# Gate/up of a SwiGLU in Strassen's form over both halves of the tokens, and a down product with the contraction outermost

## The reference

```python
def swiglu(h, w_gu, w_down):
    g, u = jnp.split(h @ w_gu, 2, axis=-1)
    return (jax.nn.silu(g) * u) @ w_down
```

## Time and profile before

| | |
|---|---|
| median of 3 runs | 1446.25 us (1444.8 to 1448.13) |
| span of the profiled execution | 1446.7 us |
| TensorE busy (matmuls) | 1404.5 us, 97% |
| weight loads | 1149.9 us, 79% |
| VectorE, ScalarE, GpSimd busy | 746.3, 553.0, 613.6 us |
| DMA | 156.67 MB, 108 GB/s over the span |
| granted TensorE clock, mean | 0.992 |

### The profile page before, as it was taken

One profiled execution on the slowest core, in us unless ns is written; L12 is line 12 of the kernel. 1 busy time (PEld: TensorE's weight loads), 2 busy tenths in 40 slices (PEclk: granted clock), 3 DMA queues, 4 the chain that ended last, 5 costly groups with the idle time before them and its releaser, 6 DMA issues.

```text
span 1446.7 us, 20394 instructions
## 1 busy us (share of the span) xinstructions
PE 1404.5 (97%) x7753; PEld 1149.9 (79%) x7753; DVE 746.3 (52%) x1023; ACT 553.0 (38%) x864; POOL 613.6 (42%) x291
## 2 busy tenths in 40 slices
PE   5999999999998999999999999999999999999997
PEld 1589667899987888888788888888888888888886
DVE  6764657893946887447745542145446411120122
ACT  4672644322214777644432223232232233233221
POOL 3353122061436554383444444444445444444442
PEclk9999999999999999999999999999999999999999
DMA  9852111414203545443233333333333433332332
GB/s 325 311 174 72 50 44 29 132 30 131 59 30 103 139 137 148 147 147 100 73 94 96 88 101 101 89 94 105 94 98 91 143 101 96 94 100 82 94 100 89
DMA packets 236451, 156.67 MB, mean 108 GB/s; under 512 B 10532, under 2 KB 221874, under 8 KB 236252
## 3 DMA queue, kind: packets, MB, share of 16 engines
q1 hardware_dynamic: 234387, 148.70, 34.1%
q10 hardware_dynamic: 1992, 6.99, 1.3%
HBM read 147.25 MB, written 8.81 MB: 108 GB/s over the span
## 4 chain that ended last, share of the span: by engine, by line
PE 88%; DVE 4%; ACT 3%; issue 1%; DVEq 0%
PE ps L1925 36%; PE ps L1930 18%; PE ps L2093 11%; PE ps L2098 6%; PE ps L2256 2%; PE ps L2233 1%; PE ps L2194 1%; PE ps L2111 1%; ACT pr L998 1%; PE ps L2140 1%; PE ps L2152 1%; PE ps L1987 1%; PE ps L1974 1%; PE ps L1994 1%; PE ps L2236 1%
## 5 line engine op out<-in xcount | busy, mean ns | idle before, releaser
L1131 POOL TENSOR_TENSOR w_lo<-raw,w_hi 128x1024 fp32r<-128x1024 f32 x152 | 376.0, 2474 | 440.8 <-ACT w_hi L708 440.8
L1925 PE MATMUL ps<-hb_hi,w_hi 128*128 128x512 f32 x768 | 300.9, 392 | 1.6 <-DVE hb_lo L1791 1.6
L1925 PE MATMUL ps<-hb_lo,w_hi 128*128 128x512 f32 x768 | 299.1, 390 | 0.0
L708 ACT ACTIVATE w_hi<-raw 128x1024 fp32r<-128x1024 f32 x152 | 160.0, 1053 | 168.0 <-PE ps L1930 163.1
L1930 PE MATMUL ps<-hb_hi,w_lo 128*128 128x512 f32 x768 | 192.2, 392 | 0.0
L1151 POOL TENSOR_TENSOR w_lo<-raw,w_hi 128x1024 fp32r<-128x1024 f32 x21 | 89.1, 4245 | 219.8 <-ACT w_hi L862 219.8
L1925 PEld LDWEIGHTS ps<-hb_hi,w_hi 128*128 128x128 f32 x768 | 144.3, 188 | 33.2 <-DVE hb_lo L1791 3.4
L1930 PEld LDWEIGHTS ps<-hb_hi,w_lo 128*128 128x128 f32 x768 | 145.1, 189 | 31.7 <-issue 1.4
L1925 PEld LDWEIGHTS ps<-hb_lo,w_hi 128*128 128x128 f32 x768 | 144.3, 188 | 29.8 <-issue 0.2
L2093 PE MATMUL ps<-ha_hi,w_hi 128*128 128x512 f32 (+2 forms) x432 | 163.5, 379 | 3.1 <-ACT p_hy L869 2.8
L2093 PE MATMUL ps<-ha_lo,w_hi 128*128 128x512 f32 (+2 forms) x432 | 161.2, 373 | 0.0
(11 more groups left out here) (296 smaller groups left out, 2107.2 us busy)
## 6 DMA issues: line engine op xcount, KB each, us to landing
raw<-in_ffn_w_gu SPq DMA_DIRECT2D x88, 512.0 KB, 3.8
ada1x<-in_ada_w SPq DMA_DIRECT2D x32, 512.0 KB, 3.9
raw<-in_ffn_w_down SPq DMA_DIRECT2D x32, 512.0 KB, 3.8
raw<-in_w_in SPq DMA_DIRECT2D x22, 512.0 KB, 4.0
ada<-in_ada_w SPq DMA_DIRECT2D x4, 2048.0 KB, 21.8
raw<-in_w_out SPq DMA_DIRECT2D x16, 512.0 KB, 3.8
raw<-in_ffn_w_down SPq DMA_DIRECT2D x16, 384.0 KB, 3.3
raw<-in_ktab SPq DMA_DIRECT2D x8, 512.0 KB, 5.8
```

The lines of the kernel that those rows point to most:

```text
L708: act.activation(w_hi[:, b, :], raw[:, b, :], ACT.Copy).then_inc(hi_done, 1)
L1131: pool.tensor_tensor(w_lo[:, b, :], raw[:, b, :], w_hi[:, b, :].bitcast(F32), ALU.subtract).then_inc(lo_done, 1)
L1925: pe.matmul(dst, w_hi[:, b, k * P:(k + 1) * P], x, start=start and i_ == 0 and n == 0, stop=False)
```

## The change

**Gate/up.** Gate and up columns of a tile, the two halves of the contraction (features 0 to 511 and 512 to 1023) and the two halves of the tokens form a 2 x 2 by 2 x 2 product. It is now done with 7 block products of 12 matmuls instead of 8. Two of the seven need the first half of the tokens only and run in a first pass over all 22 tiles (`first_half`). Their results go to DRAM: `p1_d` (first product, copied by ScalarE, `first_copy`) and `cg_d` (sum of both, by VectorE, `first_sum`). Then each of 22 rounds u does five products (`pair_product`) of sums of weight blocks with sums of input blocks. The input sums are split once (`input_sums`, `input_rests`). The weight sums are made in every round by VectorE (`pair_sums`), their heads by ScalarE (`pair_head`), their rests by GpSimd (`pair_rest`), one buffer each. VectorE adds up the products and forms the activations of both halves, which go to DRAM (`act_d`).

**Down.** The first half's product has the contraction outermost: for each of 22 rows of `w_down`, 8 output blocks accumulate in all 8 PSUM banks, with the activations read back one tile at a time. The activations of the second half are read back beside it. Its product is as before. `x1` of the first half is kept in DRAM from the start of the stage to the start of the down product.

The core of the diff (of the removed lines only the heads of the loops are shown):

```diff
-            for h in range(2):
-                    with pe.Fori(0, 4) as i:
-                        for q in range(6):
-                            down_job(i, q)
+            def first_half(f, s):
+                b, J, dst = f % 2, J_PRE + f, ps[:, 4 * s + f % 2, :]
+                if f >= 2:
+                    pe.wait_ge(c_eva if s else p1_ev, (C_EVA0 if s else P1_EV0) + f - 1)
...
+            def pair_product(u, r):
+                dst = ps[:, 2 + 3 * (u % 2) + (0, 1, 2, 0, 2)[r], :]
+                if r == 0 and u >= 2:
+                    pe.wait_ge(m_ev, M_EV0 + 6 * (u - 1))
...
+                if r >= 3:
+                    pe.wait_ge(m_ev, M_EV0 + 6 * u + (2 if r == 3 else 4))
+                pe.wait_ge(wh_ok, WH_OK0 + NP * u + r + 1)
...
+            for i in range(FT):
+                J, b = J_DN + i, i % 2
+                pe.wait_ge(hi_done, J + 1)
+                pe.wait_ge(a0_lo, A0_LO0 + i + 1)
```

ScalarE, first pass (the chain is worked off behind the head of the next tile):

```diff
+            chain = {3: lambda: root(2), 5: lambda: x1_squares(1, range(3)), 6: lambda: x1_squares(1, range(3, 6)),
+                     7: lambda: x1_squares(1, range(6, 8)), 9: lambda: root(3), 13: lambda: input_sums(0),
+                     15: lambda: input_sums(1), 16: lambda: input_sums(2), 18: lambda: input_sums(3)}
+            for f in range(FT):
+                head_of(J_PRE + f + 1)
+                if f in chain:
+                    chain[f]()
+                first_copy(f)
```

VectorE, end of the first pass, and a round:

```diff
+            input_sums(0)
+            first_sum(10)
+            input_sums(1)
+            input_rests(0)
+            first_sum(11)
+            input_sums(2)
+            first_sum(12)
+            input_rests(1)
+            first_sum(13)
+            input_sums(3)
+            first_sum(14)
+            input_rests(2)
+            first_sum(15)
+            input_rests(3)
+            for f in range(16, FT - 1):
+                first_sum(f)
+            pair_sums(0)
+            first_sum(FT - 1)
...
+            def pair_sums(u):
+                g, up = raw2[:, u % 2, 0, :], raw2[:, u % 2, 1, :]
...
+                    dve.wait_ge(wl_ok, WL_OK0 + NP * u)
+                dve.tensor_tensor(s3[:], up[:, 0:HALF], g[:, 0:HALF], ALU.subtract).then_inc(s_ok, 1)
+                dve.tensor_tensor(s1[:], up[:, 0:HALF], up[:, HALF:D], ALU.add).then_inc(s_ok, 1)
+                dve.wait_ge(s_ok, S_OK0 + 4 * u + 2)
+                dve.tensor_tensor(s2[:], s1[:], g[:, 0:HALF], ALU.subtract).then_inc(s_ok, 1)
+                dve.wait_ge(s_ok, S_OK0 + 4 * u + 3)
+                dve.tensor_tensor(s4[:], g[:, HALF:D], s2[:], ALU.subtract).then_inc(s_ok, 1)
...
+            for u in range(FT):
+                if u + 1 < FT:
+                    pair_sums(u + 1)
...
+                dve.scalar_tensor_tensor(th0[:], th0[:], 1.0, cg[:, u % 2, :], ALU.add, ALU.mult).then_inc(g_ok, 1)
...
+                dve.wait_ge(prod, PROD0 + NP * u + 2)
...
+                dve.tensor_tensor(x, x, ps[:, base + 1, :], ALU.add).then_inc(m_ev, 1)
...
+                dve.tensor_tensor(ym[:], x, ps[:, base, :], ALU.add).then_inc(m_ev, 1)
...
+                dve.tensor_tensor(c22[:], ym[:], ps[:, base + 2, :], ALU.add).then_inc(m_ev, 1)
+                dve.tensor_tensor(x, x, ps[:, base + 2, :], ALU.add).then_inc(m_ev, 1)
...
+                dve.tensor_tensor(ab[0][:], ym[:], ps[:, base, :], ALU.add).then_inc(m_ev, 1)
...
+                dve.scalar_tensor_tensor(ab[0][:], th0[:], 0.5, ab[0][:], ALU.mult, ALU.mult).then_inc(a_ok, 1)
...
+                dve.tensor_tensor(c12[:], x, ps[:, base + 2, :], ALU.add).then_inc(m_ev, 1)
...
+                link(dve.scalar_tensor_tensor(th1[:], th1[:], 1.0, c12[:], ALU.add, ALU.mult))
+                dve.scalar_tensor_tensor(ab[1][:], th1[:], 0.5, c22[:], ALU.mult, ALU.mult).then_inc(a_ok, 1)
```

(`x` is the read-back first product `px`.) SyncE, from the last rounds on:

```diff
+            act_store(FT - 1, 1)
+            act1_dma(0)
+            act1_dma(1)
+            sp.wait_ge(x1_out, X1_OUT0 + 16)
+            sp.wait_ge(prod, PROD0 + NP * FT)
+            sp.dma_start(x1h[0][:].rearrange("p k n -> p (k n)"), x1_d).then_inc(x1_ld, 16)
+            for i in range(FT):
+                if i + 2 < FT:
+                    rows_dma(i + 2)
+                    act0_dma(i + 2)
+                    act1_dma(i + 2)
```

More of the change, by code:

```diff
@@ L1122, in _ @@
+            act.wait_ge(a1_lo, A1_LO0 + FT)
+            for j in range(23):
+                head_of(J_D2 + j + 1)
+                if j == 0:
+                    x1_columns(0)
+                    x1_columns(1)
+                if j % 3 == 0 and j:
+                    down_out(j // 3 - 1)
+                if j == 3:
+                    x1_columns(2)
+                    x1_columns(3)
+                if j == 4:
+                    root(4)
+            down_out(7)
             act.wait_ge(n_var, 6)
@@ new lines, in input_rests @@
+            def input_rests(j):
+                for r in range(4):
+                    dve.wait_ge(th_ok, TH_OK0 + NP * j + r + 1)
+                    dve.tensor_tensor(t_lo[r][:, j, :], tsum[:, j % 2, r, :], t_hi[r][:, j, :].bitcast(F32), ALU.subtract).then_inc(tl_ok, 1)
+                dve.wait_ge(th_ok, TH_OK0 + NP * j + 5)
+                dve.scalar_tensor_tensor(t_lo[4][:, j, :], u1[:, 4 + j, :], mod[:, 28 + j, 0:1], t_hi[4][:, j, :].bitcast(F32),
+                                         ALU.add, ALU.subtract).then_inc(tl_ok, 1)
@@ new lines, in first_half @@
+            def first_half(f, s):
+                b, J, dst = f % 2, J_PRE + f, ps[:, 4 * s + f % 2, :]
+                if f >= 2:
+                    pe.wait_ge(c_eva if s else p1_ev, (C_EVA0 if s else P1_EV0) + f - 1)
+                elif s == 0:
+                    pe.wait_ge(acc_free, E_OUT + 16 + 2)
+                pe.wait_ge(hi_done, J + 1)
+                for k in range(4 * s, 4 * s + 4):
+                    if f == 0:
+                        pe.wait_ge(n_hl, k + 1)
+                    for x in (hb_hi, hb_lo):
+                        pe.matmul(dst, w_hi[:, b, k * P:(k + 1) * P], x[:, k, :], start=k == 4 * s and x is hb_hi, stop=False)
+                pe.wait_ge(lo_done, J + 1)
+                for k in range(4 * s, 4 * s + 4):
+                    ins = pe.matmul(dst, w_lo[:, b, k * P:(k + 1) * P], hb_hi[:, k, :], start=False, stop=k == 4 * s + 3)
+                ins.then_inc(job_done if s else p1_ps, 1)
@@ new lines, in _, with head, tail @@
+            for u in range(FT):
+                for r in range(NP):
+                    pair_product(u, r)
+            for i in range(FT):
+                J, b = J_DN + i, i % 2
+                pe.wait_ge(hi_done, J + 1)
+                pe.wait_ge(a0_lo, A0_LO0 + i + 1)
+                def head(m):
+                    if i == 0 and m == 0:
+                        pe.wait_ge(p1_ev, P1_EV0 + FT)
+                    if i == 0 and m == 2:
+                        pe.wait_ge(m_ev, M_EV0 + 6 * (FT - 1))
+                    if i == 0 and m == 5:
+                        pe.wait_ge(m_ev, M_EV0 + 6 * FT)
+                    for x in (a0h, a0l):
+                        pe.matmul(ps[:, m, :], w_hi[:, b, m * P:(m + 1) * P], x[:, b, :], start=i == 0 and x is a0h, stop=False)
+                def tail(m):
+                    return pe.matmul(ps[:, m, :], w_lo[:, b, m * P:(m + 1) * P], a0h[:, b, :], start=False, stop=i == FT - 1)
+                if i < FT - 1:
+                    for m in range(KT):
+                        head(m)
+                    pe.wait_ge(lo_done, J + 1)
+                    for m in range(KT):
+                        ins = tail(m)
+                else:
+                    pe.wait_ge(lo_done, J + 1)
+                    for m in M_LAST:
+                        head(m)
+                        ins = tail(m)
+                        if m != M_LAST[-1]:
+                            ins.then_inc(y0_ps, 1)
+                ins.then_inc(job_done, 1)
```

766 lines of the change are left out of this document (472 added, 294 removed).

## The result

The changed kernel takes 1515.09 us (median of 4 runs, 1513.78 to 1517.09) against 1447.19 for the kernel before: a ratio of 1.0475, 95% interval 1.0458 to 1.0491. It is slower by 68 us. The prediction, 1444.5 with a range of 1424 to 1468, was wrong.

A forecast was written before the change was run, and what follows sets the result against it. TensorE, busy in 97% of the span, was taken to bound the kernel. The terms -59.8 + 21.5 + 7.5 + 19 + 10.1 = -1.7 gave 1444.5 us from a profiled span of 1446.7, less 0.4 to the median; range 1424 to 1468.

The forecast's parts named there:

- What bounds, and what is removed: Whole kernel: TensorE bounds; gate/up loses 264 matmuls at 0.227 us each, 59.8 us less.
- First pass, 21.5: First pass over 22 tiles: three stops for first_sum, 14.7, norm chain 2, slow clock 4.8; 21.5 us lost.
- the norm chain: First pass, second half of the tokens: table load and reciprocal cost about 2 us, before turn 11 and at first_sum(10).
- First round, 7.5: First round: 0.9 at the start, product 4 waiting for ym, and clock 1.6; 7.5 us lost.
- Rounds 1 to 20, 19: Rounds 1 to 20: product 4 waits for ym, 14.55 us a round, 0.95 x 20 = 19 us lost.
- its rest gets in once, before s4: Each of rounds 1 to 20: one GpSimd rest holds VectorE ahead of s4, so a round takes 14.55 us.
- gets in after every VectorE operation: Rival for the rounds: a second GpSimd rest between s4 and g adds 1.2 a round, +24, 1468 us; chance 0.13.
- An idle of 1 us costs no clock: Rounds 1 to 20: TensorE's wait ahead of product 4 was priced with no slow clock behind it.
- Start of the down product, 10.1: First down product, row 2: its weights queue behind 3.4 MB; 8.5 us stop plus 1.6 of clock, 10.1 us.
- At nothing: Output projection Squares, x1 store, head of the stage and VectorE's y0 work, all taken as covered at no cost.
- The rivals: Three alternatives: GpSimd does not get in (0.25), gets in after every VectorE operation (0.13), clock falls in the rounds (0.10).
- the clock: Rival: clock falls in half of 20 rounds at 1.6 more, +16, or first pass loses 35; 1458 to 1462; chance 0.10.

The follow-up runs named there:

- the better version: Against the version with all three orders: GpSimd rests of down-product rows 0 and 1 made in quarters over eight rounds, row 2 weights loaded three rounds before the end; 1402.57 us.
- the version with all three orders: Against the changed kernel: pair_sums moved behind the adds TensorE waits for, first_sum ahead of the input operations before it, x1 loaded behind row 6's weights; 1412.57 us.
- the run with the adds first: Against the changed kernel: only pair_sums of the next round moved behind the adds TensorE waits for on VectorE; 1436.21 us.

## Why the prediction was wrong, point by point

- **What bounds, and what is removed.** Right. 7489 matmuls, at the same pitch of 0.227 when the clock is full; the version with most of the waits gone is 44 us below the kernel before, so most of the 59.8 was reached and none of the runs shows the whole of it.
- **First pass, 21.5.** Right in kind, too small: about 29. The three stops stand where they were put, at `first_sum(11)`, `(13)` and `(16)`, 4.36, 4.58 and 5.88, together 14.8 against 14.7, and `first_sum(15)` just fits, as was said. What was too small is the norm chain, put at 2: turn 11 waits 2.31, and `first_sum(10)` makes a fourth stop of 3.41. The rest is the clock, which falls behind each of the four.
- **First round, 7.5.** Its waits are 1.5 at the start and 5.6 for `ym`, 7.1 against 5.8 (0.9 and 4.9). What the clock took behind them can't be separated from the slow intervals that follow.
- **Rounds 1 to 20, 19.** This is the step that failed: "its rest gets in once, before s4", 14.55 a round. It came to 17.44 on the mean, 77 us over 20 rounds of 13.6 instead of 19. Three terms are in it. The second rest gets in ahead of g, 1.2 a round or 24, as the rival "gets in after every VectorE operation" had it, with its price. "An idle of 1 us costs no clock" was true to the earlier trace rows, but the idle became 1.87, between the 1.57 that cost none and the 2.78 that did; it cost 1.6 in 14 of the 17 rounds from 925 us on, 22 us. And the GpSimd rests of rows 0 and 1 of the down product, 2.85 each in rounds 1 and 2, were missing from the walk; with the clock behind the first three stops they make up the last 10.7.
- **Start of the down product, 10.1.** Right: from the first to the last head matmul it takes 129.7 against 119.2 in the better version, 10.5, as one stop of 8.34 and 2.2 of clock. The price put on its cause was right in part: of the 3.4 MB, x1 was 4.7 us.
- **At nothing.** Nearly right: TensorE waits 1.0 for a copy of the output projection (`yo`, the place of the Squares) and 1.7 for y0, and nowhere for the store of x1.
- **The rivals.** Two of them came true together: GpSimd getting in again, and the clock. Each was priced as if alone (1468 and 1462). They are linked: the first lengthens the idle to where the second begins. Their sum, 24 + 22 over 1444.5, is 1491, and with 8 more for the first pass and 11 for the first three intervals it is 1510, against 1515.1 measured; the last 5 are not accounted for. The price of the second rest was right (24), and so was that of one fall of the clock (1.6); that they come together was given no chance.

## What to carry to other kernels

Put an operation that frees what TensorE waits for ahead of all bookkeeping on its engine: here one call moved on VectorE was worth 79 us, two such moves in the first pass and on SyncE 25 more. Count a GpSimd operation as one that delays a short run of two-operand VectorE operations once for each time that GpSimd is ready, not once in all. And price a wait by its length and by the clock behind it: a round with an idle of 1.87 took 15.8 us, and 17.4 where the clock fell behind it, and useless matmuls in place of the idle made the kernel 24 us faster.

## What the runs showed of the hardware

- GpSimd, once ready, was let in within one VectorE operation when it came up to 3.52 us into a gap-free run of additions not yet held (one every 0.607, so ahead of the seventh), and only after the end of the run when it came at 3.60 us or later.
- The granted clock depends on more than the length of one idle. One of 1.87 us was followed by the drop in 14 of 17 rounds, and not in 3. In the version with all three orders, idles of 1.53 in two rounds were followed by a granted clock of 1.00 (857 to 871, 871 to 887). Behind one of 3.95, 14 matmuls had a pitch of 0.43 instead of 0.227, about 3 us.
- VectorE at 91%, ScalarE at 31% and GpSimd at 58% beside it left TensorE at 100% and full clock for 100 us, with 442 matmuls of 512 columns (the run with the adds first).
